# Neighbourhood attention in items of two heads by 16 grid columns, tokens stored by column

## The chip, the cores and the metric

The kernel runs on one core of a Trainium2 chip. The metric is device time in microseconds (us), the median of several executions; lower is better. Engine names: PE is TensorE, PEld its weight load, DVE is VectorE, ACT is ScalarE, POOL is GpSimd, SP is SyncE, which here only issues DMAs.

## What is computed

Two layers of a trunk over 256 latent tokens (a grid of 4 rows by 64 columns) and 256 context tokens, width 1024. Each layer is FFN, token mixer, FFN. The mixer has three branches (retention, neighbourhood attention, Fourier), gated and summed. The change is about the second:

```python
def neighbourhood_attention(q, k, v, kc, vc, rpb, rows):
    kh = min(NA_KH_MAX, rows)                      # 4 rows: all of them
    col_start = jnp.clip(cols - NA_KW // 2, 0, GRID_W - NA_KW)
    col_idx = col_start[:, None] + jnp.arange(NA_KW)[None, :]     # 16 of 64 columns
    ...
        s_loc = jnp.einsum('bhqd,bhiqjd->bhqij', qr, kn) * scale + bias
        s_ctx = jnp.einsum('bhqd,bhmd->bhqm', qr, kc) * scale
        p = jax.nn.softmax(concatenate([s_loc, s_ctx]))
        return p_loc @ vn + p_ctx @ vc
```

There are 8 heads of 64. A latent query sees 4 rows by 16 columns of keys around its own column, plus all 256 context keys, with a bias by row and column distance for the grid keys. A context query sees the 256 context keys (in the first layer only; the last layer's context output isn't needed).

## The kernel before

Everything is written out by hand per engine, with semaphores; each engine runs its list in order. Nearly all time goes to dense products: `form_a` and `token_form` (lines 1648 to 1650) multiply each weight tile three times, as high and low halves of float32r. Weights come by SP in units of 512 KB into a ring of 4 (`raw`); ACT rounds each unit to `wh` (L590), DVE subtracts to get `wl` (L1031), and PE uses both. So PE has up to four units ready.

In `mixer`, after retention and Fourier, PE forms nk and nq (units `na_in`), ACT copies nq into a tile whose other head's half is zero (L875), and PE forms nv (ACT copies it, L883; GpSimd zeroes the other head's half first, L998). Then `attention` runs a list of items in a software pipeline, one item a step on every engine:

- PE `scores` (L2000): 128 queries of one head against 512 keys (grid item, s = 0: 256 latent + 256 context) or 256 keys (context item, s = 1), into one of 3 PSUM banks.
- DVE `maximum`: adds the bias (L1479, grid items), reduces the maximum (L1480), negates it (L1481).
- ACT: exponential with sum (L798). DVE `invert`: reciprocal (L1468), scaling (L1470).
- PE `turned` (L2009): transposes of 128 keys each, 3 steps later; ACT copies them (L792).
- PE `values` (L2021): one matmul for each 128 keys, 4 steps behind `scores`, into bank 4 or 5, one bank for a pair of heads.
- When a pair of heads is done, ACT rounds the bank to `ah` (L812) and DVE subtracts to `al` (L1501).

Layer 0 has 32 items: for each of 4 pairs of heads, 4 grid items and 4 context items. Layer 1 has 16 grid items. In the last four steps ACT and DVE also round and split the first four units of the merge; after the last `scores`, PE runs one unit of it (7th bank). The keys are 4 x 64 latent columns of which a query needs 4 x 16; `wmask` puts -1e30 on the rest.

The bias table goes to DRAM in the first FFN (`tables`, L748: each row of 31 values padded to 128), and `load_bias` (L441) reads it back with a shifting offset, 4 DMAs a head: heads 0 to 3 by ACT ahead of `na_in`, heads 4 to 7 by SP inside attention, each when an earlier head's buffer is free. GpSimd adds `wmask` to each (L1004).

```python
for r in range(ROWS):
    row = (l * NH + h) * RPB_R + 7 - r
    src = bass.AP(tab.tensor, offset=row * TAB, ap=[[1, GRID_W], [TAB, ROWS], [1, GRID_W]])
```

## Time and profile before

| what | value |
|---|---|
| runs, median of 3 | 2395.88 us (2394.78 to 2396.07) |
| profiled execution, its own time | 2395.65 us |
| its span in the profile | 2393.8 us |
| PE busy | 2349.0 us (98%) |
| DVE busy | 1614.8 us (67%) |
| ACT busy | 965.4 us (40%) |
| POOL busy | 126.1 us (5%) |
| DMA traffic | 396.26 MB, mean 166 GB/s |

Busy time is the sum of instruction times; matmuls are pipelined, so a busy PE is not PE at its peak. A row of the timeline gives the start and the length of an instruction; because instructions overlap, the cost of one in a steady stream is the distance between starts. Attention runs from about 710 to 777 us (layer 0) and from 1997 to 2044 us (layer 1).

### The profile page before, as it was taken

How to read it: one execution, taken by the hardware profiler on the slowest of the kernel's cores; microseconds unless marked ns; L12 is line 12 of the kernel's file. 1: busy time of each engine (PE TensorE's matmuls, PEld its weight loads, DVE VectorE, ACT ScalarE, POOL GpSimd, SP SyncE). 2: the span in 40 equal slices, each digit the busy share in tenths (PEclk: the TensorE clock that was granted, in tenths of full speed). 3: DMA queues.
4: the chain of work that ended last, by engine and by line, in shares of the span. 5: the costliest groups of instructions: out<-in, count | busy, mean ns of one | idle time of the engine just before them, and what ended most of it. 6: DMA issues, size and time to landing. Idle time of an engine off the chain costs nothing.

```text
span 2393.8 us, 33087 instructions
## 1 busy us (share of the span) xinstructions
PE 2349.0 (98%) x13244; PEld 2033.4 (85%) x13244; DVE 1614.8 (67%) x2135; ACT 965.4 (40%) x1453; POOL 126.1 (5%) x158
## 2 busy tenths in 40 slices
PE   7999999999999999999999999999999999999998
PEld 4888988998877888898889888889889896998996
DVE  7667658856377545686766786766688556778656
ACT  3422356743126322353224464224557323544443
POOL 1000001101100000010000110000010010000000
PEclk9999999999999999999999999999999999999999
DMA  8655555651233444444556575456556243686763
GB/s 291 183 171 166 193 194 165 196 178 63 52 109 88 126 130 139 152 140 154 168 172 200 175 222 161 158 178 191 185 184 205 89 132 102 214 254 194 222 202 124
DMA packets 466300, 396.26 MB, mean 166 GB/s; under 512 B 34132, under 2 KB 418148, under 8 KB 465892
## 3 DMA queue, kind: packets, MB, share of 16 engines
q1 hardware_dynamic: 450704, 386.98, 51.6%
q10 hardware_dynamic: 15444, 7.17, 1.1%
q8 instruction: 105, 1.72, 0.3%
q14 instruction: 47, 0.39, 0.0%
HBM read 392.93 MB, written 1.17 MB: 165 GB/s over the span
## 4 chain that ended last, share of the span: by engine, by line
PE 89%; DVE 8%; issue 1%; DMA 1%; ACT 1%; ACTq 0%; POOL 0%; SPq 0%; DVEq 0%
PE ps L1648 27%; PE ps L1649 27%; PE ps L1650 27%; DVE wl L1031 2%; PE ps L1945 1%; PE ps L2021 1%; DMA araw<-in_ada_w 1%; PE ps L2104 1%; DVE st L1099 1%; PE ps L2000 1%; PE ps L1926 1%; DVE acc L1046 1%; PE ps L1755 1%; ACT wh L590 1%; DVE nms L1480 1%
## 5 line engine op out<-in xcount | busy, mean ns | idle before, releaser
L1031 DVE TENSOR_TENSOR wl<-raw,wh 128x1024 fp32r<-128x1024 f32 x560 | 681.7, 1222 | 560.4 <-ACT wh L590 558.8
L590 ACT ACTIVATE wh<-raw 128x1024 fp32r<-128x1024 f32 x560 | 591.5, 1059 | 1147.0 <-PE ps L1650 1070.3
L1648 PE MATMUL ps<-hh,wh 128*128 128x256 f32 (+1 forms) x2720 | 884.0, 325 | 1.1 <-DVE hl L1204 0.7
L1649 PE MATMUL ps<-hl,wh 128*128 128x256 f32 (+1 forms) x2720 | 880.3, 324 | 0.0
L1650 PE MATMUL ps<-hh,wl 128*128 128x256 f32 (+1 forms) x2720 | 880.2, 324 | 0.0
L1648 PEld LDWEIGHTS ps<-hh,wh 128*128 128x128 f32 x2720 | 517.8, 190 | 43.5 <-issue 1.7
L1650 PEld LDWEIGHTS ps<-hh,wl 128*128 128x128 f32 x2720 | 517.7, 190 | 40.8
L1649 PEld LDWEIGHTS ps<-hl,wh 128*128 128x128 f32 x2720 | 517.9, 190 | 40.3
L1046 DVE SCALAR_TENSOR_TENSOR acc<-araw,c,acc 128x1024 f32<-128x1024 f32 x210 | 258.6, 1280 | 54.3 <-DMA araw<-in_ada_w 52.8
L1648 PE MATMUL ps<-wh,stage_h_f 128*128 128x512 f32 x616 | 240.7, 391 | 2.0 <-DVE stage_l_f L1288 2.0
L1649 PE MATMUL ps<-wl,stage_h_f 128*128 128x512 f32 x616 | 239.8, 389 | 0.0
L1650 PE MATMUL ps<-wh,stage_l_f 128*128 128x512 f32 x616 | 239.8, 389 | 0.0
L1648 PEld LDWEIGHTS ps<-wh,stage_h_f 128*128 128x128 f32 x616 | 115.7, 188 | 28.0 <-DVE wl L1031 4.3
L1650 PEld LDWEIGHTS ps<-wh,stage_l_f 128*128 128x128 f32 x616 | 115.6, 188 | 24.2
L1649 PEld LDWEIGHTS ps<-wl,stage_h_f 128*128 128x128 f32 x616 | 115.7, 188 | 23.4
L951 POOL TENSOR_SCALAR mv<-mv 128x1 f32<-128x1 f32 x35 | 32.9, 941 | 1438.1 <-DVE mv L1105 1438.0
L1648 PE MATMUL ps<-wh,hh 128*128 128x512 f32 x192 | 76.6, 399 | 0.1
L1650 PE MATMUL ps<-wh,hl 128*128 128x512 f32 x192 | 74.8, 389 | 0.0
L1649 PE MATMUL ps<-wl,hh 128*128 128x512 f32 x192 | 74.8, 389 | 0.0
L1288 DVE TENSOR_TENSOR stage_l_f<-g,stage_h_f 128x256 fp32r<-128x256 f32 x154 | 64.4, 418 | 0.0
L646 ACT ACTIVATE stage_h_f<-g 128x256 fp32r<-128x256 f32 x154 | 61.6, 400 | 0.0
L610 ACT ACTIVATE tB<-ps,modT 128x128 f32<-128x128 f32 x156 | 56.4, 467 | 4.9 <-PE ps L1755 4.3
(201 smaller groups left out, 2325.2 us busy)
## 6 DMA issues: line engine op xcount, KB each, us to landing
raw<-in_ffa_w SPq DMA_DIRECT2D x204, 512.0 KB, 4.2
raw<-in_ffb_w SPq DMA_DIRECT2D x168, 512.0 KB, 4.2
raw<-in_mix_w_in SPq DMA_DIRECT2D x148, 512.0 KB, 4.3
araw<-in_ada_w SPq DMA_DIRECT2D x136, 512.0 KB, 5.1
raw<-in_ret_w_out SPq DMA_DIRECT2D x16, 512.0 KB, 4.6
raw<-in_na_fou_w_out SPq DMA_DIRECT2D x16, 512.0 KB, 4.0
raw<-in_mix_w_o SPq DMA_DIRECT2D x16, 512.0 KB, 3.9
raw<-in_ada_w SPq DMA_DIRECT2D x8, 512.0 KB, 5.3
```

The source lines that it names most:

```text
L590: A.activation(w_home(u)[0], raw[:, s, :], ACT.Copy).then_inc(w_rounded, 1)
L610: ins = A.activation(tB[:, t % 2, k * P:(k + 1) * P], y[:, k], ACT.Identity, scale=modT[:, i % 2, 1, k, s:s + 1], bias=modT[:, i % 2, 0, k ...
L646: A.activation(sh_[:, q % slots(i)], src[:, k0, half * SEQ:(half + 1) * SEQ], ACT.Copy).then_inc(stage_hi, 1)
L951: link(G.tensor_scalar(m[:, 1:2], m[:, 1:2], EPS, None, ALU.add))
L1031: V.tensor_tensor(low, raw[:, s, :], f(high), ALU.subtract).then_inc(w_split, 1)
L1046: ins = V.scalar_tensor_tensor(out=acc[:, st], in0=araw[:, m % AR], scalar=c, in1=acc[:, st], op0=ALU.mult, op1=ALU.add)
L1099: ins = V.bn_stats(st[:, which, t % 2, 6 * k:6 * k + 6], src[:, k * 512:(k + 1) * 512])
L1288: V.tensor_tensor(sl_[:, q % slots(i)], src[:, k0, half * SEQ:(half + 1) * SEQ], f(sh_[:, q % slots(i)]), ALU.subtract).then_inc(stage_lo, 1)
L1480: link(V.tensor_reduce(nmax[:, t % 3, 0:1], y[:, 0:key_n(items[t])], AXX, ALU.max))
L1648: T.matmul(out, a[0], b[0], start=start, stop=False)
L1649: T.matmul(out, a[0], b[1], start=False, stop=False)
L1650: return T.matmul(out, a[1], b[0], start=False, stop=stop)
```

## The change

Tokens are stored by grid column (column major, 4 rows together): x, ctx and out are read and written with `by_column`, and the constants that depend on position (rope, DFT, distances, mask) are made for that order. So 32 neighbouring columns are 128 consecutive keys. An item is now (pair of heads, s, j): both heads of the pair, 64 queries each, against

- s = 0: the 128 keys of 32 columns that hold the windows of grid columns 16j to 16j+15 (window starts 0, 8, 24, 32), and the 256 context keys;
- s = 1: the 256 context keys, for 64 context queries of each head.

nq holds the two heads' queries side by side with zeros across, so no zeros are needed in nv. The value product gives both heads' dims for both heads' queries; `out_blocks` picks the two blocks that count. nv gets two tiles more, windows 1 and 2, put together by four DMAs inside SBUF (`NV_PARTS`). A bank of outputs holds four items, so there are 8 evictions in layer 0 and 4 in layer 1, each in two pieces of 64 partitions. The bias table is stored as 16 shifted rows of 4 windows of 32, written by 8 DMAs of 1920 pieces of 32 values; a head's bias is then one DMA, all heads are loaded before attention, and the mask is added per pair of heads.

```diff
+QC, WC = 16, 32
+NQ = GRID_W // QC
+WIN = tuple(min(max(QC * j - 8, 0), GRID_W - WC) for j in range(NQ))
+LOCAL = WC * ROWS
...
-            nv = sb("nv", [P, NT, NH, P], scope=s)
+            nv = sb("nv", [P, NQ + LT, 4 * P], scope=s)
...
-        n_items = [[(2 * pr + a, s, q) for pr in range(NH // 2) for s in range(2 if l < DEPTH - 1 else 1) for q in range(LT) for a in range(2)]
-                   for l in range(DEPTH)]
+        n_items = [[(pr, s, j) for pr in range(NH // 2) for s in range(2 if l < DEPTH - 1 else 1) for j in range(NQ)] for l in range(DEPTH)]
...
+        NV_PARTS = [(j, src, max(ROWS * (WIN[j] - w), 0), min(ROWS * (WIN[j] + WC - w), P), max(ROWS * (w - WIN[j]), 0))
+                    for j in range(1, NQ - 1) for src, w in ((0, WIN[0]), (NQ - 1, WIN[-1]))]
+        def out_blocks(y, outs, item, a):
+            pr, s, _ = item
+            p = slice(DH * a, DH * a + DH)
+            if s:
+                y = y[p].rearrange("p (j b q) -> p b j q", b=2, q=DH)[:, a]
+                return y, [o[p, pr, SEQ:TOK].rearrange("p (j q) -> p j q", q=DH) for o in outs]
+            y = y[p].rearrange("p (j b r c) -> p b j r c", b=2, r=ROWS, c=QC)[:, a]
+            return y, [o[p, pr, 0:SEQ].rearrange("p (j c r) -> p j r c", r=ROWS, c=QC) for o in outs]
...
+        def pad_window(l, j):
+            v = pad[:, l, 48 + WIN[j] - QC * j:48 + WIN[j] - QC * j + WC]
+            return bass.AP(v.tensor, offset=v.offset, ap=[v.ap[0], [1, QC], [1, WC]])
         def load_bias(queue, l, h):
...
+            row = (l * NH + h) * RPB_R + RPB_R // 2 - (ROWS - 1)
+            src = bass.AP(tab.tensor, offset=row * QC * NQ * WC, ap=[[NQ * WC, ROWS * QC], [QC * NQ * WC, ROWS], [1, NQ * WC]])
+            queue.dma_start(bias[DH * (h % 2):DH * (h % 2) + DH, h // 2], src).then_inc(bias_in[h // 2], 16)
...
+                sp.wait_ge(r_fin, r0[l] + len(r_items[l]))
+                sp.wait_ge(tab_in, 16 * DEPTH * NQ)
                 for h in range(4, NH):
-                    sp.wait_ge(n_max, n0[l] + len(n_items[l]) // 4 * (h // 2 - 2) + 3 + h % 2)
                     load_bias(sp, l, h)
...
-                        act.dma_start(tab[l].rearrange("h r c -> (h r) c"), pad[:, l, :]).then_inc(tab_in, 16)
+                        for j in range(NQ):
+                            act.dma_start(tab[l, :, :, j * WC:(j + 1) * WC], pad_window(l, j)).then_inc(tab_in, 16)
...
-                    if t >= 5 and (t - 4) % (2 * per) == 0:
-                        pr = (t - 4) // (2 * per) - 1
-                        act.wait_ge(n_out, b + 2 * per * (pr + 1))
-                        A.copy(ah[:, pr, 0:N], ps[:, 4 + pr % 2, 0:N]).then_inc(n_hi, 1)
+                    if t >= 5 and (t - 4) % NQ == 0:
+                        grp = (t - 4) // NQ - 1
+                        act.wait_ge(n_out, b + NQ * (grp + 1))
+                        for a in range(2):
+                            y, o = out_blocks(ps[:, 4 + grp % 2], (ah,), items[NQ * grp], a)
+                            ins = A.copy(o[0], y)
+                        ins.then_inc(n_hi, 1)
...
+                    A.copy(nv[:, (0, NQ - 1, NQ, NQ + 1)[t]], ps[:, t]).then_inc(nv_copied, 1)
+                    if t == 1:
+                        act.wait_ge(nv_copied, NT * l + 2)
+                        for j, src, p0, p1, q0 in NV_PARTS:
+                            act.dma_start(nv[q0:q0 + p1 - p0, j], nv[p0:p1, src]).then_inc(nv_window, 16)
...
-                        link(V.tensor_tensor(y[:, 0:SEQ], y[:, 0:SEQ], bias[:, h % 4, q], ALU.add))
+                        w = y[:, 0:LOCAL].rearrange("p (c r) -> p r c", r=ROWS)
+                        link(V.tensor_tensor(w, w, bias[:, pr, :, j * WC:(j + 1) * WC], ALU.add))
...
+                        T.matmul(bank[:, 0:LOCAL], q, nk[:, pr, ROWS * WIN[j]:ROWS * WIN[j] + LOCAL], start=True, stop=True)
+                        T.matmul(bank[:, LOCAL:LOCAL + CTX], q, nk[:, pr, SEQ:TOK], start=True, stop=True).then_inc(n_score, 1)
...
-                    kts = list(range(NT) if s == 0 else range(LT, NT))
+                    kts = ([j] if s == 0 else []) + [NQ, NQ + 1]
```

**How instructions move.** On PE at the start of layer 0's attention (`nk,nq` are scores, `ident,prob` transposes, `probT,nv` values), before:

```order
L2000 MATMUL ps<-nk,nq 128x512 x4
L2009 MATMUL ps<-ident,prob 128x128 x4
L2000 MATMUL ps<-nk,nq 128x256
L2009 MATMUL ps<-ident,prob 128x128 x4
L2021 MATMUL ps<-probT,nv 128x128 x4
L2000 MATMUL ps<-nk,nq 128x256
L2009 MATMUL ps<-ident,prob 128x128 x4
```

and with the change, from the fourth grid item's scores on:

```order
L2025 MATMUL ps<-nk,nq 128x128
L2026 MATMUL ps<-nk,nq 128x256
L2036 MATMUL ps<-ident,prob 128x128 x3
L2028 MATMUL ps<-nk,nq 128x256
L2036 MATMUL ps<-ident,prob 128x128 x3
L2049 MATMUL ps<-probT,nv 128x128 x3
L2028 MATMUL ps<-nk,nq 128x256
```

Each grid item's scores become two matmuls, 128 and 256 columns; its transposes and value matmuls go from four to three.

On DVE in layer 0, at the first grid items of the second pair of heads (`al` is the eviction of an output bank, `bias` an add), before:

```order
L1479 TENSOR_TENSOR ps<-ps,bias 128x256
L1480 TENSOR_REDUCE nms<-ps 128x1
L1481 TENSOR_SCALAR nms<-nms 128x1
L1468 RECIPROCAL nms<-nms 128x1
L1470 TENSOR_SCALAR prob<-prob,nms 128x256
L1479 TENSOR_TENSOR ps<-ps,bias 128x256
L1480 TENSOR_REDUCE nms<-ps 128x1
L1481 TENSOR_SCALAR nms<-nms 128x1
L1468 RECIPROCAL nms<-nms 128x1
L1470 TENSOR_SCALAR prob<-prob,nms 128x512
```

and with the change:

```order
L1500 TENSOR_TENSOR ps<-ps,bias 128x4x32
L1501 TENSOR_REDUCE nms<-ps 128x1
L1502 TENSOR_SCALAR nms<-nms 128x1
L1488 RECIPROCAL nms<-nms 128x1
L1490 TENSOR_SCALAR prob<-prob,nms 128x256
L1524 TENSOR_TENSOR al<-ps,ah 64x4x4x16 x2
L1500 TENSOR_TENSOR ps<-ps,bias 128x4x32
L1501 TENSOR_REDUCE nms<-ps 128x1
L1502 TENSOR_SCALAR nms<-nms 128x1
L1488 RECIPROCAL nms<-nms 128x1
L1490 TENSOR_SCALAR prob<-prob,nms 128x384
```

An eviction of two pieces now stands also between grid items, where there was none; adds are 128 columns in four runs.

On ACT in the first FFN (`rpb_table` is the bias table in DRAM), before:

```order
L721 ACTIVATE sgf<-ps 128x512
L745 DMA lgt<-in_ret_decay_logit 128x16
L748 DMA rpb_table<-tA 120x128 x2
L590 ACTIVATE wh<-raw 128x1024 x2
L721 ACTIVATE sgf<-ps 128x512
```

and with the change:

```order
L742 ACTIVATE sgf<-ps 128x512
L766 DMA lgt<-in_ret_decay_logit 128x16
L770 DMA rpb_table<-tA 1920x1x32 x8
L611 ACTIVATE wh<-raw 128x1024 x2
L742 ACTIVATE sgf<-ps 128x512
```

Two stores of 120 rows become eight of 1920 pieces, at the same place.

## Rows read from the trace of the kernel before

**Rows 1.** The page, part 4: the chain that ended last, by engine

```profile
PE 89%; DVE 8%; issue 1%; DMA 1%; ACT 1%; ACTq 0%; POOL 0%; SPq 0%; DVEq 0%
```

**Rows 2.** Timeline of TensorE, layer 1's attention: start us, us, engine, line, op, operands

```profile
2005.86 0.60 PE L2009 MATMUL ps<-ident,prob 128*128 128x128 f32 x4
2006.29 1.06 PE L2021 MATMUL ps<-probT,nv 128*128 128x128 f32 x8
2007.19 1.02 PE L2000 MATMUL ps<-nk,nq 128*128 128x512 f32 x2
2008.05 0.60 PE L2009 MATMUL ps<-ident,prob 128*128 128x128 f32 x4
```

**Rows 3.** Timeline of VectorE, layer 0's attention, one grid item

```profile
741.55 0.42 DVE L1479 TENSOR_TENSOR ps<-ps,bias 128x256 f32<-128x256 f32 x1
742.01 0.69 DVE L1480 TENSOR_REDUCE nms<-ps 128x1 f32<-128x512 f32 x1
742.74 0.15 DVE L1481 TENSOR_SCALAR nms<-nms 128x1 f32<-128x1 f32 x1
...
743.40 0.43 DVE L1479 TENSOR_TENSOR ps<-ps,bias 128x256 f32<-128x256 f32 x1
```

**Rows 4.** Timeline of VectorE, layer 0's attention, an eviction among context items

```profile
745.69 0.15 DVE L1481 TENSOR_SCALAR nms<-nms 128x1 f32<-128x1 f32 x1
...
747.00 0.69 DVE L1501 TENSOR_TENSOR al<-ps,ah 128x512 fp32r<-128x512 f32 x1 [0.56 <-ACT ah L812]
747.61 0.41 DVE L1480 TENSOR_REDUCE nms<-ps 128x1 f32<-128x256 f32 x1
748.06 0.15 DVE L1481 TENSOR_SCALAR nms<-nms 128x1 f32<-128x1 f32 x1
...
748.58 0.42 DVE L1480 TENSOR_REDUCE nms<-ps 128x1 f32<-128x256 f32 x1
```

**Rows 5.** Timeline of VectorE, bias adds that begin a grid item, both layers

```profile
711.15 0.43 DVE L1479 TENSOR_TENSOR ps<-ps,bias 128x256 f32<-128x256 f32 x1 [2.94 <-PE ps L2000]
...
724.17 0.43 DVE L1479 TENSOR_TENSOR ps<-ps,bias 128x256 f32<-128x256 f32 x1 [0.90 <-PE ps L2000]
...
751.44 0.43 DVE L1479 TENSOR_TENSOR ps<-ps,bias 128x256 f32<-128x256 f32 x1 [0.81 <-PE ps L2000]
...
1998.19 0.43 DVE L1479 TENSOR_TENSOR ps<-ps,bias 128x256 f32<-128x256 f32 x1 [10.04 <-PE ps L2000]
...
2027.88 0.43 DVE L1479 TENSOR_TENSOR ps<-ps,bias 128x256 f32<-128x256 f32 x1
...
2032.16 0.43 DVE L1479 TENSOR_TENSOR ps<-ps,bias 128x256 f32<-128x256 f32 x1
```

**Rows 6.** Groups by shape, ScalarE: line, op, shapes, count | busy us, mean ns | idle

```profile
L798 ACT ACTIVATE prob<-ps,nms 128x512 f32<-128x512 f32 x32 | 22.0, 688 | 33.2 <-DVE nms L1481 32.1 <-PE ps L2009 1.1
...
L875 ACT ACTIVATE nq<-ps 64x256 f32<-64x256 f32 x16 | 6.0, 377 | 0.2
```

**Rows 7.** Timeline of ScalarE, first FFN and the nv copies of layer 0

```profile
191.26 0.20 ACT L752 ACTIVATE small<-lgt 128x16 f32<-128x16 f32 x1
...
702.09 0.65 ACT L883 COPY nv<-ps 128x256 f32<-128x256 f32 x2 [6.55 <-PE ps L1650]
```

**Rows 8.** Instructions on the tensor rpb_table: durations ns min/median/max, first and last start

```profile
L748 ACTq DMA_DIRECT2D rpb_table<-tA x2: 432/442/453, 157.7 to 158.2; - x2
```

**Rows 9.** DMA queues, 645 to 656 us: packets, MB, share of 16 engines

```profile
q10 hardware_dynamic: 2977, 0.72, 31.0%
```

**Rows 10.** Four stretches: us, busy and count by engine, granted clock, DMA share, GB/s

```profile
764.00:766.00 2.00, 0.61 (x3) 0.38 (x4) 0.88 (x2) 1.77 (x4) 0.00 (x0) 1.00 0.58 173
768.00:770.00 2.00, 2.00 (x7) 1.62 (x6) 1.35 (x2) 0.88 (x2) 0.00 (x0) 0.51 0.82 241
2030.00:2034.00 4.00, 1.69 (x12) 1.26 (x12) 2.88 (x6) 1.93 (x4) 0.00 (x0) 1.00 0.40 119
180.00:200.00 20.00, 20.00 (x90) 16.54 (x90) 17.16 (x23) 5.76 (x9) 0.00 (x0) 1.00 0.48 157
```

More of the change, by code:

```diff
@@ L380, in trunk @@
         n0 = [0, len(n_items[0])]
+        g0 = [0, len(n_items[0]) // NQ]
+        groups = [len(items) // NQ for items in n_items]
         f0 = [0, len(f_items[0])]
@@ L782, in attention @@
                 items, b = n_items[l], n0[l]
-                per = len(items) // NH
                 for t in range(len(items) + 5):
@@ L1463, in attention @@
                 items, b = n_items[l], n0[l]
-                per = len(items) // NH
                 def invert(t):
@@ L1497, in attention @@
                         low(6, 2)
-                    if t >= 5 and (t - 4) % (2 * per) == 0:
-                        pr = (t - 4) // (2 * per) - 1
-                        dve.wait_ge(n_hi, 4 * l + pr + 1)
-                        V.tensor_tensor(al[:, pr, 0:N], ps[:, 4 + pr % 2, 0:N], f(ah[:, pr, 0:N]), ALU.subtract).then_inc(n_lo, 1)
+                    if t >= 5 and (t - 4) % NQ == 0:
+                        grp = (t - 4) // NQ - 1
+                        dve.wait_ge(n_hi, g0[l] + grp + 1)
+                        for a in range(2):
+                            y, (high, low_) = out_blocks(ps[:, 4 + grp % 2], (ah, al), items[NQ * grp], a)
+                            ins = V.tensor_tensor(low_, y, f(high), ALU.subtract)
+                        ins.then_inc(n_lo, 1)
                     if 0 <= t - (len(items) - RING) < RING:
@@ L1992, in attention @@
                 items, b = n_items[l], n0[l]
-                per = len(items) // NH
                 def scores(t):
-                    h, s, q = items[t]
+                    pr, s, j = items[t]
                     if t >= 3:
                         pe.wait_ge(n_exp, b + t - 2)
-                    c = s * SEQ + q * P
-                    T.matmul(ps[:, SCORE_BANKS[t % 3], 0:key_n(items[t])], nq[:, q_slot(h), c:c + P],
-                             nk[:, h // 2, s * SEQ:TOK], start=True, stop=True).then_inc(n_score, 1)
+                    bank = ps[:, SCORE_BANKS[t % 3]]
+                    if s == 0:
+                        q = nq[:, 0, pr, j]
+                        T.matmul(bank[:, 0:LOCAL], q, nk[:, pr, ROWS * WIN[j]:ROWS * WIN[j] + LOCAL], start=True, stop=True)
+                        T.matmul(bank[:, LOCAL:LOCAL + CTX], q, nk[:, pr, SEQ:TOK], start=True, stop=True).then_inc(n_score, 1)
+                    else:
+                        T.matmul(bank[:, 0:CTX], nq[:, 1, pr, j], nk[:, pr, SEQ:TOK], start=True, stop=True).then_inc(n_score, 1)
                 def turned(t):
@@ L2012, in values @@
                 def values(t):
-                    h, s, q = items[t]
-                    pr = h // 2
+                    pr, s, j = items[t]
+                    grp = t // NQ
                     pe.wait_ge(n_turnc, b + t + 1)
-                    if t % (2 * per) == 0 and pr >= 2:
-                        pe.wait_ge(n_lo, 4 * l + pr - 1)
-                    c = s * SEQ + q * P
-                    kts = list(range(NT) if s == 0 else range(LT, NT))
-                    for j, kt in enumerate(kts):
-                        ins = T.matmul(ps[:, 4 + pr % 2, c:c + P], nv[:, kt, h], probT[:, t % 2, j * P:(j + 1) * P],
-                                       start=j == 0 and h % 2 == 0, stop=j == len(kts) - 1 and h % 2 == 1)
+                    if j == 0 and grp >= 2:
+                        pe.wait_ge(n_lo, g0[l] + grp - 1)
+                    if s == 0 and 0 < j < NQ - 1:
+                        pe.wait_ge(nv_window, 16 * len(NV_PARTS) * (l + 1))
+                    kts = ([j] if s == 0 else []) + [NQ, NQ + 1]
+                    for m, kt in enumerate(kts):
+                        ins = T.matmul(ps[:, 4 + grp % 2, j * P:(j + 1) * P], nv[:, kt, pr * P:(pr + 1) * P], probT[:, t % 2, m * P:(m + 1) * P],
+                                       start=m == 0, stop=m == len(kts) - 1)
                     ins.then_inc(n_out, 1)
                 pe.wait_ge(nq_zero, 2 * l + 2)
-                pe.wait_ge(nv_zero, l + 1)
                 for t in range(len(items) + 4):
@@ L2194, in constants @@
     k["k_dft_n"] = np.ascontiguousarray(both.reshape(2, P, 2, SEQ).transpose(1, 0, 2, 3))
-    cq = GRID_W - 1 - np.arange(P) % GRID_W
-    start = np.clip(cq - 8, 0, GRID_W - 16)
-    ck = np.arange(GRID_W)
-    inside = (ck[None] >= start[:, None]) & (ck[None] < start[:, None] + 16)
-    k["k_wmask"] = np.where(inside, 0, -1e30).astype(f32)
-    key = (np.arange(2)[None, :, None] * P + np.arange(P)[:, None, None]).astype(f32)
-    qry = np.arange(SEQ, dtype=f32)[None, None, :]
+    tile = np.arange(NQ)
+    cq = QC * tile[None] + QC - 1 - (np.arange(P) % QC)[:, None]
+    first = np.clip(cq - 8, 0, GRID_W - 16)[:, :, None]
+    ck = (np.array(WIN)[:, None] + np.arange(WC)[None])[None]
+    inside = (ck >= first) & (ck < first + 16)
+    k["k_wmask"] = np.where(inside, 0, -1e30).astype(f32).reshape(P, NQ * WC)
+    key = pos.reshape(2, P).T[:, :, None].astype(f32)
+    qry = pos.astype(f32)[None, None, :]
     k["k_dist"] = np.ascontiguousarray(np.stack([np.maximum(qry - key, 0), np.maximum(key - qry, 0),
```

69 lines of the change are left out of this document (28 added, 41 removed).

## The prediction

> **What bounds the kernel now.** I began with the chain that ended last: 89% of it is TensorE [rows 1]. After the start, which waits for DMA, TensorE has no gap worth a term outside the two attention stages, so the change can gain or lose only in three places: the two attention stages, and wherever its new preparation holds back the engines that feed TensorE. I then read TensorE in order of time inside layer 1's attention. A grid item there (one head by 128 queries, 512 keys) takes 2.19 us back to back: transposes from 2005.86 (0.43), values from 2006.29 (0.90), scores from 2007.19 (0.86), and again [rows 2]. Last I read VectorE in the same stage. One grid item takes it 1.85 us: bias add to reduce 0.46, reduce to negation 0.73, negation to the next bias add 0.66 (in this lie the reciprocal and the scaling of the item before) [rows 3]. So a grid item is bound by TensorE (2.19 against 1.85), with VectorE close behind. A context item (256 keys) costs TensorE 1.09, half of the same parts, and VectorE 0.97: 0.45 reduce, 0.52 from negation to next reduce [rows 4].
>
> Starts of grid items on VectorE give what whole stretches took. Layer 0: the first pair of heads 13.02 (711.15 to 724.17), the next two together 27.27 (to 751.44). Layer 1: 13 items in 29.69 (1998.19 to 2027.88), then 4.28 for an item that is interleaved with rounding and splitting of the merge weights [rows 5].
>
> **The change part by part.** The number of items stays 32 and 16, of which 16 and 16 are grid items. What shrinks is the grid item: 128 + 256 keys instead of 512.
>
> TensorE, one grid item: scores 0.86 x 384/512 = 0.65 (the split into two matmuls adds a weight load; the value matmuls, which load weights for every 128 columns, run 8 records in 0.90, 0.112 each, and two such records plus two of 256 columns at 0.215 give the same 0.65), transposes 3/4 of 0.43 = 0.32, values 3/4 of 0.90 = 0.68. Sum **1.65, that is 0.54 less**.
>
> VectorE, one grid item: the bias add falls from 256 to 128 columns, reduce and scaling from 512 to 384. Slopes come from pairs of widths: reduce 0.73 and 0.45 gives 0.59 at 384; negation to next 0.66 and 0.52 gives 0.59; the add falls by 0.13 to 0.33. Sum **1.51, that is 0.34 less**. The add now steps through PSUM four elements at a time. No row shows such a step. Between no cost and twice the time for an element (128 elements, 0.13 us) I take none, since the copies into nq that already run backwards, 64x256 in 0.38 [rows 6], are no dearer than others of that size; 0.13 stays for the range.
>
> Evictions of the output bank: layer 0 had 4 of 512 columns, it gets 8, each of two 64-partition pieces of 256 columns on ScalarE and two on VectorE; layer 1 keeps 4 but each in two pieces. In the row of before, VectorE stood from the end of the scaling near 746.4 until 747.00 for ScalarE's half, then used 0.61 to 747.61 [rows 4]. From the negation of a context item (745.69) to al it is 1.31: the exponential, then the copy. Now two copies of 0.38 [rows 6] that overlap a little stand for one of 512 columns, some 0.13 more, so 1.44; where the item is a grid item its exponential has 128 columns more, at most a quarter of the 0.69 that 512 take [rows 6], and I add 0.10. VectorE has 0.5 to 0.6 of its own in that time, so it waits 0.84 to 1.0, and the two pieces take 0.34 each (0.61 at 512 columns, less 0.27 for 256 as in the reduce). **An eviction costs VectorE 1.5 to 1.7**.
>
> So the engine that bounds changes. Layer 0, a full pair of heads: TensorE 4 x 1.65 + 4 x 1.09 = 10.96; VectorE 4 x 1.51 + 4 x 0.97 + 1.5 + 1.7 = 13.1. VectorE decides: two pairs 26.2 to 26.3 instead of 27.27, 1.0 saved. The first pair has no eviction in it; VectorE needs 9.9 and TensorE 10.96 against 13.1 before, so I take 2.2 of 13.02, and 0.2 from the first scores matmul. The last pair's grid items are 4 x 1.51 + 1.7 = 7.7 against 7.4: 0.3 lost. Its context items are unchanged but for 0.2 in an eviction. Layer 0: **2.9 saved**.
>
> Layer 1: the first step is 1.05 (no scaling in it), eleven more at 1.51 are 16.6, the eviction at the ninth item 1.6, and the item with an eviction and the first rounding about 5.0 (it was as long before: shorter arithmetic, dearer eviction). That is 24.2 against 29.69, 5.5 saved. TensorE's 1.65 per item is not far above and stays hidden behind VectorE's mean of 1.9 once evictions are in. The 4.28 of the next steps fall by 0.13 + 0.14 + 0.10 (add, reduce, exponential), three times: 1.1. The last values and transposes, two items with one block less each, 0.5; the first scores 0.2. Layer 1: **7.3 saved**.
>
> Taken at nothing, with what covers each. The mask additions and bias loads that ran on GpSimd and SP inside attention move ahead of it (four loads a queue instead of sixteen): they lengthened a few VectorE scalings, which my VectorE sum already leaves out. ScalarE's queue issues 4 bias loads, not 16, before na_in; TensorE did not wait there, so nothing is gained. The four nv window copies are issued by ScalarE after the second nv copy, where it idles 6.55 us for TensorE [rows 7]; four issues cost 2 to 3 us of it. If that cover were gone, the last nv copies and so the first scores would be late by the excess. The column order of x, ctx and out keeps 4 KB rows, so those loads stay. The block of zeros in nv was never waited for.
>
> The **table write** is the one new burden. It was two stores of 120 pieces; it is now eight of 1920 pieces of 128 bytes, 15360 in all, issued by ScalarE in the first FFN at 157.7 [rows 8], and ScalarE waits for them just ahead of 191.26 [rows 7]. In 645 to 656, 2977 pieces of 256 bytes took 31.0% of 16 engines for 11 us: 18.3 ns each [rows 9]. Between half of that, by bytes, and all of it, by count, 15360 take 9 to 18 us of all 16 engines. The weight stream leaves them about half free (DMA share 0.48) [rows 10], so the write lasts 18 to 36 us and lands between 176 and 194, where the wait is at 191. ScalarE being late by up to 3 us delays nothing: it keeps four weight units of 5.4 us ahead of TensorE, 16 us and more. I take **0**, and at most that the write costs what rival C says. The Trainium skill, "DMA: Bandwidth & Descriptors", Specifications, says that transfers under 512 B are not at line rate, since the engines read, modify and write. By that rule a piece might cost double and the forecast would be rival C's.
>
> Sum: 2395.65 (the profiled execution; its span is 2393.8 and the median of the runs 2395.88, so the same within 0.25) - 2.9 - 7.3 = **2385.4**.
>
> **The rivals.** A measurement of this kernel can tell about 0.2%, 4.8 us, from no change.
>
> A, the forecast: VectorE becomes the bound and 8 to 13 us go, 2383 to 2388. For it: both sums stand on rows. Chance 0.56.
>
> B, the new shapes are dearer. If a step of four elements doubles the time for an element, each of 32 adds costs 0.13 more, and each strided piece of an eviction (16 in all on VectorE) 0.27: 8.5 in sum, of which some 6 on the bounding engine, so 2391. With a dearer ScalarE half too, up to 2396. Against it: nothing in the trace; for it: nothing either. "Advanced Engine Details and Errata" of the Trainium skill, Memory Cachelines, says that an access which meets a new line each time (16 bytes in SBUF, 8 in PSUM) pays a penalty; a step of four fp32 is such an access, and no run here shows it yet. Chance 0.22.
>
> C, slower: the table write. At 37 ns a piece, twice the row, it needs 35 us of all engines. By 191 about 17 are done; with ScalarE held, the weight loads run dry and the rest follows at full rate, to some 214. ScalarE is then 23 late, of which its lead hides 16. If its queue is also held while the eight stores are issued, it stands from 158 on, and 20 to 30 us reach TensorE: 2395.65 - 10 + 20 = **2406**, up to 2416. It decides from about 30 ns a piece, or from a landing after 205. Chance 0.10.
>
> D, more: evictions overlap better than I think, TensorE stays the bound with 1.65 and 1.09, a pair takes 11.2, and layer 0 gains 4 to 5 more: 2380. Against it: 747.00 to 747.61 shows VectorE really standing before al. Chance 0.12.
>
> The granted clock belongs to all of these. With TensorE busy 0.61 of 2 us (764 to 766) the clock still read 1.00, and at 768 to 770 it was 0.51, the lower level, under full work; in layer 1, 1.69 busy of 4 us left it at 1.00 [rows 10]. In the VectorE-bound part TensorE will be busy 85%, more than in either, so I expect no loss there; a fall near an end costs 1 to 3 us and is in the range.
>
> **How the numbers follow.** Predicted: A's 2385.4. The range 2380 to 2394 takes in A, D and most of B (0.56 + 0.09 + 0.18 = 0.83) and leaves out C and the ends. Faster by over 0.2% (under 2391.1): A, D and half of B, 0.79. Within 0.2%: the rest of B and 0.01 of C, 0.12. Slower: 0.09.
>
> **What would show it.** In the profile after, a grid item on TensorE should show scores in 0.65, three transposes, three value blocks; on VectorE a step of 1.51 between adds, and an idle of 0.8 to 1.0 ahead of each al. TensorE should now wait in mid attention for VectorE. The 13 items of layer 1 should take about 24. The sum is wrong if the strided add takes over 0.33 (B), if the rpb_table stores land later than 205 or TensorE has gaps between 158 and 230 (C), or if a pair of layer 0 takes 11 (D).

## The result, and the profile after

| | median us | runs | against before |
|---|---|---|---|
| before | 2395.95 (2394.78 to 2396.12) | 5 | |
| after | 2405.14 (2404.70 to 2406.37) | 5 | 1.0038 (1.0027 to 1.0050) |

The change made the kernel 9 us slower; the forecast was 10.2 us faster. SP's issues of the layer-norm weights stand at fixed places of the program, so their times tell where the drift arises. The four marks are the end of the first FFN's first half, the end of layer 0's mixer, the same FFN place in layer 1, and the last FFN. Issues of lnw by SP, after:

```profile
L515 SPq DMA_DIRECT2D lnw<-in_ln_w x1: 582/582/582, 284.2 to 284.2; - x1
L515 SPq DMA_DIRECT2D lnw<-in_ln_w x1: 327/327/327, 1008.2 to 1008.2; - x1
L515 SPq DMA_DIRECT2D lnw<-in_ln_w x1: 580/580/580, 1657.2 to 1657.2; - x1
L515 SPq DMA_DIRECT2D lnw<-in_ln_w x1: 579/579/579, 2311.3 to 2311.3; - x1
```

And the same of the kernel before:

```profile
L494 SPq DMA_DIRECT2D lnw<-in_ln_w x1: 581/581/581, 273.2 to 273.2; - x1
L494 SPq DMA_DIRECT2D lnw<-in_ln_w x1: 328/328/328, 995.1 to 995.1; - x1
L494 SPq DMA_DIRECT2D lnw<-in_ln_w x1: 1102/1102/1102, 1643.9 to 1643.9; - x1
L494 SPq DMA_DIRECT2D lnw<-in_ln_w x1: 580/580/580, 2302.6 to 2302.6; - x1
```

So 11.0 us are gone by the first mark, before any attention. Layer 0's stretch with attention took 724.0 instead of 721.8 (2.2 lost, where 2.9 had been forecast as saved), layer 1's 654.1 instead of 658.7 (4.6 saved, forecast 7.3).

**The first FFN.** The kernel before goes on in its rhythm behind its two table stores; its next rounding is released by TensorE:

```profile
162.62 1.06 ACT L590 ACTIVATE wh<-raw 128x1024 fp32r<-128x1024 f32 x1 [3.89 <-PE ps L1650]
```

Timeline of ScalarE and its queue (ACTq), after; the columns are start, us, engine, line, operation, operands, and in brackets the idle time ahead and what ended it:

```profile
158.01 1.06 ACT L611 ACTIVATE wh<-raw 128x1024 fp32r<-128x1024 f32 x1 [4.38 <-PE ps L1674]
158.50 1.03 ACTq L770 DMA_DIRECT2D rpb_table<-tA  x1
158.97 0.58 ACT L742 ACTIVATE sgf<-ps 128x512 f32<-128x512 f32 x1
159.56 18.82 ACTq L770 DMA_DIRECT2D rpb_table<-tA  x7
178.49 2.00 ACT L611 ACTIVATE wh<-raw 128x1024 fp32r<-128x1024 f32 x2 [18.93 <-issue]
```

Seven stores took 18.82 us to issue, 2.69 each, and ScalarE did nothing else: the idle time ahead of its next rounding is put down to "issue". Its roundings come every 5.44 us there, so the next was due at about 163.4 and came 15 us late. The eight issues differ: min, median and max in ns are

```profile
L770 ACTq DMA_DIRECT2D rpb_table<-tA x8: 1032/2360/3904, 158.5 to 176.7; - x8
```

The same moment on VectorE and on TensorE:

```profile
179.58 1.23 DVE L1052 TENSOR_TENSOR wl<-raw,wh 128x1024 fp32r<-128x1024 f32 x1 [16.25 <-ACT wh L611]
180.72 0.68 DVE L1378 TENSOR_TENSOR g<-sgf,ps 128x512 f32<-128x512 f32 x1
```
```profile
173.84 0.39 PE L1674 MATMUL ps<-hh,wl 128*128 128x512 f32 x1
181.50 0.76 PE L1672 MATMUL ps<-hh,wh 128*128 128x512 f32 x1 [7.27 <-issue]
```

TensorE stood 7.27 us and went on right when `g` was written (180.72 + 0.68): what it missed was a free PSUM bank (it waits at the head of each FFN step for the `g` of two steps back, line 1885), not weights: the unit for that step was split at 161.51 already. `g` itself was late because VectorE's list has the split of the next unit ahead of it, and that split waited 16.25 us for ScalarE's rounding. No weight load was late either, for ScalarE rounded two units back to back (178.49, x2) as soon as it was free. TensorE restarted at the lower clock. Stretches of after, with busy time of each engine, then granted clock, DMA share and GB/s:

```profile
178.00:181.00 3.00, 0.00 (x0) 0.00 (x0) 1.42 (x2) 2.51 (x4) 0.00 (x0) 0.50 0.82 108
181.00:184.00 3.00, 2.50 (x6) 2.05 (x7) 3.00 (x4) 0.92 (x1) 0.00 (x0) 0.50 0.81 203
184.00:190.00 6.00, 6.00 (x21) 4.77 (x21) 5.65 (x6) 0.08 (x1) 0.00 (x0) 0.74 0.23 64
```

Some 5.3 us of work at 1.2 GHz instead of 2.4 (matmuls 0.43 us apart instead of 0.23) are another 2.6 us: together about 10. In 158 to 178 ScalarE's ring of transfers (q10) took over half of the time of the 16 DMA engines:

```profile
q10 hardware_dynamic: 12264, 1.55, 53.5%
```

That is 0.535 x 16 x 20 us / 12264 = 14.0 ns for a piece of 128 bytes, against 18.3 for 256 in [rows 9]: within the forecast's bounds for a piece. The last store had landed by 183.

**Attention.** VectorE in layer 0, after, from the first grid item of the second pair of heads through both evictions (a pair of heads has one of each kind); this answers to [rows 3, 4]:

```profile
732.50 0.30 DVE L1500 TENSOR_TENSOR ps<-ps,bias 128x128 f32<-128x128 f32 x1 [0.47 <-PE ps L2026]
...
733.69 0.35 DVE L1490 TENSOR_SCALAR prob<-prob,nms 128x256 f32<-128x256 f32 x1
735.44 1.25 DVE L1524 TENSOR_TENSOR al<-ps,ah 64x256 fp32r<-64x256 f32 x2 [1.40 <-ACT ah L835]
736.72 0.30 DVE L1500 TENSOR_TENSOR ps<-ps,bias 128x128 f32<-128x128 f32 x1
...
738.25 0.29 DVE L1500 TENSOR_TENSOR ps<-ps,bias 128x128 f32<-128x128 f32 x1
...
739.76 0.29 DVE L1500 TENSOR_TENSOR ps<-ps,bias 128x128 f32<-128x128 f32 x1
...
743.14 0.86 DVE L1524 TENSOR_TENSOR al<-ps,ah 64x256 fp32r<-64x256 f32 x2 [0.74 <-ACT ah L835]
...
747.29 0.30 DVE L1500 TENSOR_TENSOR ps<-ps,bias 128x128 f32<-128x128 f32 x1 [0.23 <-PE ps L2026]
```

Two numbers stand beside the forecast. The grid item's step is 1.51 (738.25 to 739.76), as summed. The pair takes 14.79 (732.50 to 747.29), not 13.1: a grid eviction costs 2.7 from the end of the scaling (734.04) to the next add, with 1.40 of standing and two pieces of 0.63, a context eviction 1.6 (742.40 to 744.03). Of the context items behind it two take 0.98, VectorE's own pace, and the last 1.29 (746.00 to 747.29), since VectorE waits at its end for TensorE's scores of the next pair. ScalarE's side of the grid eviction:

```profile
734.19 1.22 ACT L835 CAST ah<-ps 64x256 fp32r<-64x256 f32 x2
```

Two pieces of 0.61 each, where I had taken 0.38. These are the pieces that go from row-by-row queries to column-by-column tokens.

### The profile page after: what moved, and what is told of

It is laid out like the page before. It is cut to its first block, busy times and chain, and to the rows that moved or that the text cites. A ratio compares the mean times of both kernels' runs of the same rounds, so it can differ in the third digit from the quotient of the medians.

```text
span 2402.9 us, 33013 instructions
## 1 busy us (share of the span) xinstructions
PE 2342.5 (97%) x13212; PEld 2034.2 (85%) x13212; DVE 1611.5 (67%) x2151; ACT 971.9 (40%) x1461; POOL 114.3 (5%) x146
## 4 chain that ended last, share of the span: by engine, by line
PE 89%; DVE 7%; issue 1%; ACT 1%; DMA 1%; POOL 0%; ACTq 0%; DVEq 0%; SPq 0%
PE ps L1672 27%; PE ps L1674 27%; PE ps L1673 27%; DVE wl L1052 1%; PE ps L1969 1%; PE ps L2131 1%; DVE st L1120 1%; PE ps L1950 1%; PE ps L1779 1%; PE ps L2049 1%; DVE nms L1501 1%; ACT wh L611 1%; DVE acc L1067 1%; PE ps L1760 0%; PE ps L2119 0%
## 5 line engine op out<-in xcount | busy, mean ns | idle before, releaser
L1674 PEld LDWEIGHTS ps<-wh,stage_l_f 128*128 128x128 f32 x616 | 115.6, 188 | 24.2
```

The lines of the kernel that those rows point to most:

```text
L1674: return T.matmul(out, a[1], b[0], start=False, stop=stop)
```

## The experiments

The kernel before was measured beside each; its median there was 2395.3 to 2395.4, so runs of different groups can be compared. Theory T: eight stores in a row hold ScalarE (about 10 us), and strided evictions make VectorE stand (what is missing in attention).

| run | median us | against before (interval) |
|---|---|---|
| e1_spread | 2394.81 | 0.9997 (0.9988 to 1.0006) |
| e2_pool | 2527.02 | 1.0551 (1.0536 to 1.0565) |
| e3_burden | 2403.54 | 1.0035 (1.0023 to 1.0047) |
| e4_token | 2389.78 | 0.9978 (0.9970 to 0.9987) |
| e5_late | 2383.06 | 0.9952 (0.9940 to 0.9965) |
| e6_both | 2380.70 | 0.9939 (0.9925 to 0.9952) |
| e7_contig | 2389.92 | 0.9977 (0.9968 to 0.9986) |
| e8_fours | 2389.26 | 0.9976 (0.9967 to 0.9985) |
| e9_before_late | 2393.35 | 0.9991 (0.9982 to 1.0000) |
| e10_few | 2395.02 | 0.9997 (0.9988 to 1.0006) |

**e1_spread: the stores one by one**

```diff
-                    for l in range(DEPTH):
-                        for j in range(NQ):
-                            act.dma_start(tab[l, :, :, j * WC:(j + 1) * WC], pad_window(l, j)).then_inc(tab_in, 16)
                 elif q == HEAD + 7 + DEPTH:
-                    act.wait_ge(tab_in, 16 * DEPTH * NQ)
...
+                elif q == HEAD + 6 + DEPTH + DEPTH * NQ:
+                    act.wait_ge(tab_in, 16 * DEPTH * NQ)
+                if HEAD + 4 + DEPTH <= q < HEAD + 4 + DEPTH + DEPTH * NQ:
+                    l, j = divmod(q - HEAD - 4 - DEPTH, NQ)
+                    act.dma_start(tab[l, :, :, j * WC:(j + 1) * WC], pad_window(l, j)).then_inc(tab_in, 16)
```

> The changed kernel with its eight table stores spread over eight steps of the first FFN, one each, and ScalarE's wait for them moved from the step of the decay logits to after the last. Pieces, bytes and source are the same. Theory T (ScalarE's queue was held while it issued eight stores of 1920 pieces in a row; 7.3 us of stand on TensorE at 181.5 and some 3 us of work at the lower clock behind it): the stand and the low clock go, 2395 (2393 to 2398), and the mark of the end of the first FFN's first phase moves from 284.2 back to about 274. Rival L (the small pieces load the 16 DMA engines or the memory, whoever issues them and whenever): the same pieces cost the same, 2403 to 2406. Rival S (the column order of x and ctx at the start costs most of the 11 us): nothing changes, 2405.

Measured: 2394.81, 10.3 under after; the first mark at 274.5. The other stretches are unchanged (724.0 and 654.1). The eight issues now take a median of 0.87 us, and there is no gap on TensorE:

```profile
L777 ACTq DMA_DIRECT2D rpb_table<-tA x8: 866/872/1028, 159.0 to 236.6; - x8
```

T holds: the same 15360 pieces cost nothing when they are not asked for in one go. Rivals L and S fall. What remains beside before is attention's account: 4.6 won, 2.2 lost, and a first mark 1.3 later than before's; that mark fell between 272.9 and 274.5 in kernels without the burst, so I read nothing into it.

**e2_pool: the stores from another queue**

```diff
             norm(0, False, True)
+            pool.wait_ge(go, 1)
+            for l in range(DEPTH):
+                for j in range(NQ):
+                    for c in range(8):
...
+                        pool.dma_start(tab[l, r, :, j * WC:(j + 1) * WC], v).then_inc(tab_in, 16)
```

> The changed kernel with the table stored at the same moment, but issued by GpSimd, which is idle then, in 64 stores of 240 pieces; ScalarE waits for the table at the same place as before. Theory T (only ScalarE's held queue costs): 2395 to 2397, unless the stores land so late that ScalarE's wait at 202 grows over its lead. Rival L (the load of small pieces itself, all within some 30 us): TensorE still stands at 181, 2403 to 2406.

Measured: 2527.02. The condition in the expectation decided: GpSimd issues one store of 240 pieces every 2.7 us (64 of them from 159.5 to 332.0), so the table was complete near 334, and ScalarE waited for it. Waits of ScalarE, then of TensorE, 150 to 420:

```profile
ACT small L773 <- DMA rpb_table<-tA: 141.4, 1, 141.4
...
PE ps L1678 <- issue: 129.6, 1, 129.6
```

TensorE had no gap until 209, while stores were already going out, but at a slower rate than in after; so this run can't tell T from L, e1 and e3 do. It does show what stands behind one wait on ScalarE: of 141.4 us, 129.6 reached TensorE. Its next rounding, due at 196.8, came at 335.9, 139.1 late, so 9.5 were hidden at this place.

**e3_burden: the kernel before, with the same eight stores**

```diff
                         act.dma_start(tab[l].rearrange("h r c -> (h r) c"), pad[:, l, :]).then_inc(tab_in, 16)
+                    for l in range(DEPTH):
+                        for j in range(4):
+                            v = pad[:, l, 16 * j:16 * j + 32]
+                            v = bass.AP(v.tensor, offset=v.offset, ap=[v.ap[0], [1, 16], [1, 32]])
+                            act.dma_start(spare[l, :, :, j * 32:(j + 1) * 32], v).then_inc(spare_in, 16)
```

> The kernel before the change, with eight more stores of 1920 pieces of 128 bytes each, behind its two table stores, into a DRAM tensor that nothing reads, and ScalarE waits for them where it waits for the table. Nothing else of the change is in it. Theory T: it loses what the change lost there, about 10 us, 2404 to 2408, with ScalarE standing while it issues and TensorE's stand near 181. If the loss in the changed kernel's first FFN came from the order of x, ctx or other loads: 2396.

Measured: 2403.54, 8.2 over before, a little under the 8.7 to 12.7 expected. ScalarE, in this run:

```profile
159.12 16.87 ACTq L755 DMA_DIRECT2D spare<-tA  x8
176.09 2.00 ACT L592 ACTIVATE wh<-raw 128x1024 fp32r<-128x1024 f32 x2 [16.86 <-issue]
```

Held for 2 us less, so TensorE stood 5.2 instead of 7.3. Its next rounding was due near 163.1 and came 13.0 late: 7.8 hidden, 5.2 not. In after 15.0 late, 7.3 not hidden: 7.7. The lead of ScalarE, that is by how much it can be late before TensorE stands, is the same in both. This trace is of the fastest of six runs (2401.22, 5.9 over before), so its 5.2 us of standing belong to less than the median's 8.2.

**e10_few: the same bytes in larger pieces**

```diff
-                            v = pad[:, l, 16 * j:16 * j + 32]
-                            v = bass.AP(v.tensor, offset=v.offset, ap=[v.ap[0], [1, 16], [1, 32]])
-                            act.dma_start(spare[l, :, :, j * 32:(j + 1) * 32], v).then_inc(spare_in, 16)
+                            v = tA[0:NH * RPB_R, 0, 0:DEPTH * TAB]
+                            v = bass.AP(v.tensor, offset=v.offset, ap=[v.ap[0], [0, 2], [1, 256]])
+                            act.dma_start(spare[l, j], v).then_inc(spare_in, 16)
```

> The kernel before the change with the same eight extra stores and bytes (245,760 each) as the burden kernel, but in 240 pieces of 1 KB each instead of 1920 of 128 bytes. Theory T (ScalarE is held while it issues by the number of pieces that its queue has to take): each issue takes 0.4 to 0.6 us, ScalarE is held some 4 us, nothing reaches TensorE, 2395 to 2396. Rival W (what holds the queue is the bytes or the number of stores in a row): each issue takes 1.7 us and more as with small pieces, 2403.

Measured: 2395.02, no cost. Each issue took more than T said (median 0.87, eight in 7.35 us), still a third of 2.69, so T's 4 us of hold were too few. The next rounding was due near 161.9 (5.44 after the one ahead of the sigmoid at 157.39) and came 3.4 late, inside the lead of 7.7:

```profile
157.86 7.35 ACTq L755 DMA_DIRECT2D spare<-tA  x8
165.31 1.06 ACT L592 ACTIVATE wh<-raw 128x1024 fp32r<-128x1024 f32 x1 [7.34 <-issue]
```

So neither bytes nor the number of stores held the queue, but small pieces in a row: a single store of 1920 pieces issues in 0.87 (e1), in a row of seven or eight they average 2.1 to 2.7. That a store waits until pieces of the last ones have left is inferred from paces, not shown: in after the seven stores were issued at 714 pieces a us, and from 160 to 176 the ring moved 10468, or 654 a us. By 178, 12264 had left of the 15360 asked for, so some 3100 stood in the queue; e10's eight stores have 1920 pieces in all. At what number the hold begins was not measured.

**e8_fours: two groups of four** (on the token-order kernel below)

```diff
-                if HEAD + 4 + DEPTH <= q < HEAD + 4 + DEPTH + DEPTH * NQ:
-                    l, j = divmod(q - HEAD - 4 - DEPTH, NQ)
+                for l, j in [(l, j) for l in range(DEPTH) for j in range(NQ) if q == HEAD + 4 + DEPTH + 3 * l]:
```

> The token-order kernel with the eight table stores in two groups of four, three steps of the first FFN apart, instead of one per step. Theory T with the lead as after's trace shows it (TensorE can go two steps on after ScalarE's last sigmoid, and stood from 174.2 when ScalarE had been held since 159.6 and its next work was due at 162.4: a lead of some 9 us and a chain of 3 behind the release): each group holds ScalarE about 9 us, which the lead just hides, 2389.8 to 2391. Rival Q (any held queue reaches TensorE in proportion): half of the loss of eight in a row for each group, 2395 to 2400.

Measured: 2389.26, the same as one by one. ScalarE was held 7.46 and then 2.99 + 4.31, and TensorE has no gap from 150 to 250. ScalarE's next rounding, due at 164.2, came 3.1 late, the one behind the second group 3.7. Lateness below the lead costs nothing, so rival Q falls; between 3.7 and 13.0 us late there is no run. In this kernel the table lies in another order in DRAM, and a store that meets an empty queue issues in 0.32 us instead of 0.87 (e4's median of eight), with as many pieces; why is open. In a row it is held as before (three in 7.46); the expectation's 9 us of hold and lead were both too large.

```profile
159.72 7.46 ACTq L776 DMA_DIRECT2D rpb_table<-tA  x3
167.28 1.06 ACT L611 ACTIVATE wh<-raw 128x1024 fp32r<-128x1024 f32 x1 [6.99 <-issue]
```

**e4_token: queries in token order**

```diff
-            y = y[p].rearrange("p (j b r c) -> p b j r c", b=2, r=ROWS, c=QC)[:, a]
-            return y, [o[p, pr, 0:SEQ].rearrange("p (j c r) -> p j r c", r=ROWS, c=QC) for o in outs]
+            y = y[p].rearrange("p (j b q) -> p b j q", b=2, q=DH)[:, a]
+            return y, [o[p, pr, 0:SEQ].rearrange("p (j q) -> p j q", q=DH) for o in outs]
...
-                            ins = A.activation(o[:, 0].rearrange("p j (r c) -> p j c r", r=ROWS)[:, :, ::-1, ::-1],
-                                               y[:, 0:SEQ].rearrange("p (j c r) -> p j c r", c=QC, r=ROWS), ACT.Copy, scale=DH ** -0.5)
+                            ins = A.activation(o[:, 0, :, ::-1],
+                                               y[:, 0:SEQ].rearrange("p (j q) -> p j q", q=DH), ACT.Copy, scale=DH ** -0.5)
```

> The spread table again, and the 64 queries of a grid item in the order in which tokens are stored (column, then row) instead of row by column: the eviction pieces of grid items and the copies into nq are then contiguous runs of 64, with the bias rows, the mask and the table's layout in the same order. Number and width of all instructions are the same. Theory T (a grid eviction costs VectorE 2.7 us instead of 1.7 because its 64x4x4x16 pieces take 0.61 on ScalarE and 0.63 on VectorE): each of eight grid evictions gives back about 1.0 us, of which all on VectorE's path but the last one or two: 6 to 8 us under the spread kernel, about 2388. Rival N (what costs is the number of pieces, not their stride): the same as the spread kernel, 2395. Rival G (layer 0 lost to the lower clock at its end): 0 to 2 us less than the spread kernel, 2393.

Measured: 2389.78, 5.0 under the spread kernel; T said 6 to 8. A grid eviction now stands 0.91 and its two pieces take 0.86, so 0.88 less each, not 1.0. Timeline of VectorE, e4_token, one pair of heads:

```profile
721.77 0.30 DVE L1501 TENSOR_TENSOR ps<-ps,bias 128x128 f32<-128x128 f32 x1 [0.47 <-PE ps L2027]
...
724.22 0.86 DVE L1525 TENSOR_TENSOR al<-ps,ah 64x256 fp32r<-64x256 f32 x2 [0.91 <-ACT ah L836]
...
735.68 0.30 DVE L1501 TENSOR_TENSOR ps<-ps,bias 128x128 f32<-128x128 f32 x1 [0.23 <-PE ps L2027]
```

The pair falls from 14.8 to 13.91. By the marks (273.4, 995.5, 1644.4, 2296.7) layer 0's stretch gave 1.9 and layer 1's 1.8; the other 1.1 lies before the first mark, within the spread that this mark has between kernels. So the attention stages gave 3.7, well under T. The stride itself, by all instructions of ScalarE's half, in after and in e4_token:

```profile
L835 ACT CAST ah<-ps x24: 352/601/632, 734.2 to 2054.6; 64x256 fp32r<-64x256 f32 x24
```
```profile
L836 ACT CAST ah<-ps x24: 352/367/368, 723.5 to 2039.7; 64x256 fp32r<-64x256 f32 x24
```

Same 64 x 256 elements, 601 ns as the median (16 of the 24 pieces are strided in after) against 367. Rivals N and G fall: number of pieces and order of items are unchanged.

**e7_contig: the bias add without its step in PSUM**

```diff
-                        w = y[:, 0:LOCAL].rearrange("p (c r) -> p r c", r=ROWS)
+                        w = y[:, 0:LOCAL].rearrange("p (r c) -> p r c", r=ROWS)
```

> The token-order kernel, whose bias add reads and writes the 128 columns in PSUM one after the other instead of four apart; each score thus gets the bias of another key (part of the computation is changed). Rival B of the prediction (a step of four elements in PSUM costs): the add falls from 0.293 us to 0.16 to 0.20, and the time by 2 to 4 us from 2389.8. Theory T: the add stays at 0.29 and the time at 2389.8, within 1.

Measured: 2389.92, the same as e4_token. The 32 adds of e7_contig, then those of e4_token, where each element lies four apart:

```profile
L1501 DVE TENSOR_TENSOR ps<-ps,bias x32: 290/293/300, 712.0 to 2030.8; 128x128 f32<-128x128 f32 x32
```
```profile
L1501 DVE TENSOR_TENSOR ps<-ps,bias x32: 290/293/300, 711.2 to 2031.0; 128x128 f32<-128x128 f32 x32
```

To the nanosecond the same. In PSUM this step costs VectorE nothing in an add of 128 x 128.

**e5_late and e6_both: VectorE's half of the eviction one item later**

```diff
-                    if t >= 5 and (t - 4) % NQ == 0:
+                    if t >= 6 and (t - 5) % NQ == 0 or t == len(items) + 4:
                         grp = (t - 4) // NQ - 1
                         dve.wait_ge(n_hi, g0[l] + grp + 1)
```

> The spread kernel, with VectorE's half of each eviction (al) moved one item later, behind the next item's maximum and scaling; the pieces stay strided. Theory T (in layer 0's attention VectorE stands 1.40 us for ScalarE at each grid eviction and 0.74 at each context eviction, and this is on the path): of seven evictions in layer 0 and three in layer 1 each gives back what it stood, as far as TensorE's 10.96 us per pair of heads allows: 6 to 10 us under the spread kernel's 2394.8, about 2387. Rival P (TensorE or ScalarE takes over at once as the bound, since the pair is a chain that alternates between engines): 0 to 3 us under it, 2392 to 2395.

> The spread kernel with the queries of grid items in token order and with the later al. Theory T: VectorE needs 4 x 1.51 + 4 x 0.97 + 2 x 0.86 = 11.6 us per pair of heads and stands for nothing, against 13.9 in the token-order kernel: 2.3 for each of three pairs, some 1 in the last and 2 in layer 1, 8 to 10 us under its 2389.8, about 2381. Rival P: TensorE's 10.96 and the handovers between the engines take most of it, 2386 to 2389.

Measured: 2383.06 for e5 (11.7 under the spread kernel, more than T's 10) and 2380.70 for e6 (9.1 under e4, inside T's range). No `al` waits any more in the middle of attention, and the pair is down to 12.23. Timeline of VectorE, e6_both:

```profile
722.45 0.30 DVE L1501 TENSOR_TENSOR ps<-ps,bias 128x128 f32<-128x128 f32 x1 [0.47 <-PE ps L2027]
...
725.42 0.85 DVE L1525 TENSOR_TENSOR al<-ps,ah 64x256 fp32r<-64x256 f32 x2
...
734.68 0.30 DVE L1501 TENSOR_TENSOR ps<-ps,bias 128x128 f32<-128x128 f32 x1 [0.38 <-PE ps L2027]
```

With e5 the marks put the gain where it had been missing: layer 0's stretch takes 716.8 (990.1 less 273.3), 5.0 under before, and layer 1's 651.4 (2290.8 less 1639.4), 7.3 under. Beside e1 that is 7.2 and 2.7, so 9.9 in attention, inside T's range; 1.2 more lie before the first mark.

What bounds a pair now? Four pieces of the chain that ended last, e6_both, 722 to 747 (start, us, what). Apart from 0.01 to 0.03 of issue now and then, only VectorE stands in it from 722.45 to 727.92, and only TensorE from 727.97 to 734.66:

```profile
727.49 0.43 DVE prob L1491
727.97 0.55 PE ps L2037 x3
...
734.21 0.45 PE ps L2027 x2
734.68 0.31 DVE ps L1501
```

So neither engine bounds alone. VectorE sets the time while it works on the grid items (5.5 us), and TensorE in the rest of the pair (6.7 us), which makes 12.2 where TensorE's sum is 10.96 and VectorE's 11.6. VectorE stands only 0.38 us in it.

e6_both beats both kernels: 15 us under before and 24 under after.

**e9_before_late: the same edit in the kernel before**

```diff
-                    if t >= 5 and (t - 4) % (2 * per) == 0:
+                    if t >= 6 and (t - 5) % (2 * per) == 0 or t == len(items) + 4:
                         pr = (t - 4) // (2 * per) - 1
```

> The kernel before the change, with VectorE's half of each eviction one item later, as in the later-al kernels. It has four evictions of 512 columns in layer 0 and four of 256 in layer 1. Theory T (before, TensorE bounds a grid item with 2.19 us against VectorE's 1.85, so that standing for ScalarE is mostly covered, and the change moved the bound to VectorE, where the same edit gave 11.7): 0 to 2 us under 2395.3. Rival V (standing for ScalarE is on the path in both kernels, and the later al is worth the same whatever the items' shape): 4 us and more under it, 2391.

Measured: 2393.35, 2.1 less (the interval just reaches no change), at the edge of T's range, and 11.7 in the changed kernel. How long VectorE stood for ScalarE at its half of the evictions in the whole kernel (us, times, longest), before and after (e1 stands as long as after, 11.2):

```profile
DVE al L1501 <- ACT ah L812: 4.1, 4, 1.5
```
```profile
DVE al L1524 <- ACT ah L835: 11.3, 9, 2.3
```

The chain of before, 724 to 752, shows the cover in the middle of layer 0's attention, with TensorE nearly alone in it:

```profile
by line: PE ps L2021 40.6%; PE ps L2000 38.6%; PE ps L2009 19.6%; DVE nms L1480 2.5%; DVE ps L1479 1.6%; issue 0.4%
```

There e9 takes away two stands of 0.56, and two pairs of heads take 26.93 instead of 27.27, so two thirds of the 1.12 had been covered. By the marks 1.8 of the gain are in layer 0 (720.1 instead of 721.9), most of it at the end, where a stand of 1.51 fell away; layer 1 gave nothing for its stand of 1.46. Two things thus make 2.1 into 11.7: the change took cover away (half of 4.1 came back before, all of 11.2 after), and it made the standing itself longer by some 7 us, with eight evictions instead of four in layer 0 and strided pieces. The second is the larger. Of e6's 15 us some 2 could have been had without the change.

## Why the prediction was wrong

**The table write: the step "I take 0" failed.** Its size was near (14.0 ns a piece, landed by 183, inside the 9 to 18 us and 176 to 194 of the sum), and the wait that I priced, ScalarE's for the table, cost nothing beyond. What I didn't price in the forecast was the issue: ScalarE can't compute while its queue is held, and it was held for 18.82 us. The measured price of the term is 10.3 us (after against e1). It stood in rival C as a second clause. C's time, 2406, was met within 1 us with a chance of 0.10, and largely by luck: C's first clause, 37 ns a piece and a landing near 214, did not happen (and by its own numbers, 17 of 35 us done by 191, it gives 209); by C's reckoning the table cost 20 and attention gave 10, and measured, the table cost 10.3 and attention gave about 2. The Trainium skill, "DMA: Bandwidth & Descriptors", Specifications, puts pieces under 512 B below line rate. The trace agrees by bytes: 128 in 14.0 ns are 9.1 a ns, 256 in 18.3 are 14.0. The doubling of a piece's cost that I drew from it is not in the trace.

**"ScalarE keeps four weight units ahead, 16 us and more" failed.** Measured lead: 7.7 us (after, e3), 9.5 at e2's place. The weights of the next step were there; the PSUM banks of the FFN step ran out first, because VectorE's product that frees one stands in its list behind the split that waits for ScalarE. And a stand has a second part that I only priced at an end of attention: 2.6 us of the lower clock behind it.

**VectorE's item arithmetic was right.** Step 1.51 forecast and measured, the add 0.33, no cost for the step in PSUM (e7); first pair of heads 10.60 (721.90 to 732.50), which is what 13.02 - 2.2 - 0.2 gives; TensorE's grid item 1.65 forecast, 1.66 measured (scores of layer 1 start at 2018.12, then at 2019.78).

**"An eviction costs VectorE 1.5 to 1.7" failed for the grid evictions**, which cost 2.7. I took 0.38 for ScalarE's piece from the nq copies [rows 6], which wrote runs; the new piece writes SBUF 16 bytes apart and takes 0.61, VectorE's 0.63 instead of 0.34. Rival B had this (0.27 a piece supposed, 0.21 to 0.24 measured) but I weighed it as one with the step in PSUM, which costs nothing. The nq copies were strided by the change as well: 646 ns as the median in after, 379 in e4. The trace thus agrees with "Advanced Engine Details and Errata" of the Trainium skill, Memory Cachelines, for SBUF (a penalty when each access meets a new line). What the page says of PSUM it says of matmuls; VectorE's add there pays nothing (293 ns both ways). Token order took back 5.0 us (e4), 3.7 of it in the attention stages.

**"VectorE decides: 13.1 for a pair" missed 14.8.** The excess of 1.7 is 1.0 in the grid eviction, some 0.1 in the context eviction, and 0.5 in the four context items, which took 4.4 instead of 3.9. The step that failed is that one engine's column bounds the pair: e6's chain passes from VectorE to TensorE within a pair and takes 12.2, above both columns (11.6 and 10.96). So rival D, 11.2 for a pair, was out of reach even without a single stand for ScalarE. The first pair won what was forecast; the next two took 29.60 (732.50 to 762.10) against 27.27, 2.3 lost; the last pair and what follows up to the mark lost 2.5, forecast 0.5. Of that 1.5 are in its grid items (8.76 against 7.26); the rest was not separated.

**Layer 1:** 13 items took 26.75, forecast 24.2, before 29.69. The item with the first eviction has 1.1 of the excess (2.7 for the eviction instead of 1.6), the one with the second and the first rounding 1.4 (6.4 instead of 5.0; VectorE stands 2.26 there). Near its end the clock, forecast as a matter for the range, read 0.55 from 2040 to 2045 and 0.77 to 2050, after stands of 1.49 and 2.07 us on TensorE; before, it stayed at 1.00 there. What that cost by itself was not separated from the stands.

## What to carry to other kernels

Price a DMA by who issues it: count the pieces, and ask what the issuing engine owes in the time it is held; then find the shortest reserve behind it (PSUM banks here, not weights). Bursts that made ScalarE up to 3.7 us late were free (e8, e10); at 13 and 15 us late, all above 7.7 counted. When an edit takes work off the engine that bounds, list the waits which that engine's slack had covered, and the new ones that the edit makes: one line, VectorE's half an item later, was worth 2.1 us before the change and 11.7 after it. Where two kinds of items alternate, add the bound kind by kind and look at the chain, not at the two columns. Keep the order in which a result is stored as the order in which it is computed, and put a step, where there must be one, on the PSUM side (shown for VectorE's add of 128 x 128).
